# Chunked gated DeltaNet scan: solving for the residue of values and state product instead of for keys and values apart, with the keys' sums in other banks

## What is computed

```python
m = where(strict, (kb @ k.T) * decay, 0)          # kb = k * beta
a = m + eye(L)
sol = triangular_solve(a, [v * beta, kb * exp(G)])
w_val, k_cd = sol[:dv], sol[dv:]
def step(st):                                      # chunk after chunk
    v_new = w_val - k_cd @ st
    o = (q * exp(G)) @ st + attn @ v_new
    st = st * g_tot + k_tail.T @ v_new
```

## Time and profile before

| | |
|---|---|
| runs | 3146.82 us median of 3 (3145.96 to 3149.22) |
| the profiled execution | 3142.87 us, of which 3141.1 us are the span shown |
| busy in the span | PE 96%, PEld 92%, DVE 51%, POOL 35%, ACT 23% |
| granted clock of PE, mean | 0.981 of full speed |
| the scan | about 1821 to 2191 us of the span |

### The profile page before, as it was taken

One profiled execution on the slowest core, in us unless ns is written; L12 is line 12 of the kernel. 1 busy time (PEld: TensorE's weight loads), 2 busy tenths in 40 slices (PEclk: granted clock), 3 DMA queues, 4 the chain that ended last, 5 costly groups with the idle time before them and its releaser, 6 DMA issues. The chain is left out here.

```text
span 3141.1 us, 52954 instructions
## 1 busy us (share of the span) xinstructions
PE 3009.7 (96%) x22592; PEld 2885.3 (92%) x22592; DVE 1595.7 (51%) x2718; ACT 722.8 (23%) x1413; POOL 1089.4 (35%) x731
## 2 busy tenths in 40 slices
PE   8999999999999999999999969996999999999995
PEld 7999668999999999999999958885999999999995
DVE  2338665744444334478666645563473344433456
ACT  2213473310110100123221235553121001101012
POOL 2233101253222332327532147774452322322330
PEclk9999999999999999999999989997999999999998
DMA  6120102011111111114323134321311111111111
GB/s 173 45 62 7 48 1 85 14 54 45 43 41 41 48 54 48 41 28 126 98 84 97 59 104 110 89 69 54 94 39 41 54 48 41 43 46 41 48 41 57
DMA packets 265152, 185.48 MB, mean 59 GB/s; under 512 B 49833, under 2 KB 249879, under 8 KB 264919
## 3 DMA queue, kind: packets, MB, share of 16 engines
q1 hardware_dynamic: 264919, 182.11, 19.7%
HBM read 148.24 MB, written 33.84 MB: 58 GB/s over the span
## 5 line engine op out<-in xcount | busy, mean ns | idle before, releaser
L148 PE MATMUL ps<-xhi,whi 128*128 128x364 f32 (+1 forms) x3504 | 1159.7, 331 | 18.8 <-POOL wlo L1417 15.0
L149 PE MATMUL ps<-xlo,whi 128*128 128x364 f32 (+1 forms) x3504 | 1154.6, 330 | 0.0
L154 PE MATMUL ps<-xhi,wlo 128*128 128x364 f32 (+1 forms) x3504 | 1153.6, 329 | 0.0
L148 PEld LDWEIGHTS ps<-xhi,whi 128*128 128x128 f32 (+1 forms) x3504 | 659.1, 188 | 24.1 <-POOL wlo L1417 16.6
L149 PEld LDWEIGHTS ps<-xlo,whi 128*128 128x128 f32 (+1 forms) x3504 | 659.5, 188 | 3.2 <-issue 0.3
L154 PEld LDWEIGHTS ps<-xhi,wlo 128*128 128x128 f32 (+1 forms) x3504 | 658.8, 188 | 1.4
L1414 POOL TENSOR_SCALAR whi<-wraw 128x1024 fp32r<-128x1024 f32 x168 | 189.7, 1129 | 1235.6 <-PE ps L154 1235.3
L1980 DVE TENSOR_TENSOR z<-ps,z 128x364 f32<-128x364 f32 x432 | 232.0, 537 | 575.2 <-PE ps L154 575.2
L1417 POOL TENSOR_TENSOR wlo<-wraw,whi 128x1024 fp32r<-128x1024 f32 x168 | 431.6, 2569 | 14.0
L148 PE MATMUL ps<-eo_hhi,whi 128*128 128x364 f32 x528 | 174.5, 331 | 0.0
L148 PE MATMUL ps<-oo_hhi,whi 128*128 128x364 f32 x528 | 174.2, 330 | 0.0
(11 more groups left out here) (405 smaller groups left out, 4408.3 us busy)
## 6 DMA issues: line engine op xcount, KB each, us to landing
wraw<-in_w_ff_in SPq DMA_DIRECT2D x88, 512.0 KB, 3.7
wraw<-in_w_ff_out SPq DMA_DIRECT2D x44, 512.0 KB, 3.4
qkvz<-eo_ob SPq DMA_DIRECT2D x32, 546.0 KB, 4.6
wraw<-in_w_in_o SPq DMA_DIRECT2D x32, 512.0 KB, 4.5
z<-residual SPq DMA_DIRECT2D x6, 1456.0 KB, 8.2
wraw<-in_w_in_e SPq DMA_DIRECT2D x17, 512.0 KB, 3.9
residual<-z SPq DMA_DIRECT2D x3, 1456.0 KB, 6.7
dn_gb<-gates SPq DMA_DIRECT2D x34, 128.0 KB, 3.4
```

Of the source, the lines that this page charges most:

```text
L148: one = pe.matmul(out, whi, xhi, start=start, stop=False)
L149: two = pe.matmul(out, whi, xlo, start=False, stop=False)
L154: return pe.matmul(out, wlo, xhi, start=False, stop=stop)
```

## The change

It replaces the two products at the stage's end. Instead of TT applied to scaled keys and to scaled values, the recurrence forms the residue r = v - (k exp(G)) S first (DVE, `residue`), applies TT to it (PE, `solve`), and multiplies by beta (DVE, `new_values`). beta therefore sits in the rows of `upl`/`ups` and the columns of `low` differently (POOL's `pre` swaps two factors). The scaled keys `kc` are made by POOL (`scaled_keys`) from the normalised keys and `eg`. ACT copies the turned values in one instruction into `vt`. TT, `vt` and `kc` are double. The keys' sums go to banks 4 and 5, the turned values to 6 and 7. Ln of B's output norm is taken at level 3 (`root_o`), Exp and `normed` at level 4, and Exp for the mask `upi` is moved from level 2 to 3. The setup of `bcol` is dropped. The diff, cut, with eight columns of indentation removed:

```diff
-kbg, vb, kc, vn, Sg = (sb(n, [P, H, P]) for n in ("kbg", "vb", "kc", "vn", "Sg"))
+vt = (sb("vt0", [P, H, P]), sb("vt1", [P, H, P]))
+kc = (sb("kc0", [P, H, P]), sb("kc1", [P, H, P]))
+vn, Sg = (sb(n, [P, H, P]) for n in ("vn", "Sg"))
 ktl = (sb("ktl0", [P, H, P]), sb("ktl1", [P, H, P]))
 S = (sb("S0", [P, H, P]), sb("S1", [P, H, P]))
 egl = sb("egl", [P, 2, 2, H])
+TT = (TT, sb("TT1", [P, H, L]))
...
-            sp.wait_ge(s("ups_b"), A.th(1, 1))
+            sp.wait_ge(s("low_b"), A.th(1, 1))
...
+            sp.wait_ge(s("kc"), A.th(1, 1))
...
+    def scaled_keys(A):
+
+        pool.wait_ge(s("kn"), A.th(1, 1))
+        pool.wait_ge(s("eg"), A.th(1, 1))
+        if A.k >= 2:
+            pool.wait_ge(s("kS"), A.th(-2, 2))
+        for b, r in enumerate(A.blocks()):
+            ins = pool.tensor_tensor(kc[A.odd][:, :, r].rearrange("p (g hh) c -> p g hh c", g=2),
+                                     kk[:, b].rearrange("p hh g c -> p g hh c"),
+                                     eg[:, b].rearrange("p (g hh) c -> p g hh c", g=2), ALU.mult)
+        ins.then_inc(s("kc"), 1)
+
     def run(A, B, C):
         if B:
             decayed(B, 0)
         if A:
+            scaled_keys(A)
             levels_of(A, (1,))
...
-        pe.wait_ge(s("Tv"), B.th(1, 1))
+        if not B.first:
+
+            pe.wait_ge(s("oln"), B.th(0, 1))
...
+    def solve(B, b):
+
+        pe.wait_ge(s("r"), B.th(b + 1, 2))
+        pe.wait_ge(s("TT"), B.th(B.group(LEVELS - 1, b), 2 * LEVELS))
+        for h, half, j in places(b):
+            ins = pe.matmul(bank2(0)[half, j, :], TT[B.odd][half, j, :], vt[B.odd][half, j, :], start=True, stop=True)
+        ins.then_inc(s("Tr"), 1)
...
-            pe.wait_ge(s("vb"), A.th(1, 1))
+            pe.wait_ge(s("kln"), A.th(1, 1))
...
-                ins = pe.matmul(bank2(6)[:, HALVES[b], :], m.ones[:, :], sq[:, HALVES[b], :],
+                ins = pe.matmul(bank2(4)[:, HALVES[b], :], m.ones[:, :], sq[:, HALVES[b], :],
                                 start=True, stop=True)
             ins.then_inc(s("ksum"), 1)
             pe.wait_ge(s("in2"), A.loaded())
             if not A.first:
-                pe.wait_ge(s("kc"), A.th(0, 1))
-            turn(A, 4, kv, "vturned")
+                pe.wait_ge(s("TT"), A.th(0, 2 * LEVELS))
+            turn(A, 6, kv, "vturned")
         if B:
             old_values(B, 0)
+            solve(B, 0)
         if A:
             pe.wait_ge(s("kn"), A.th(1, 1))
+            pe.wait_ge(s("vt"), A.th(1, 1))
             gram_k(A)
...
             old_values(B, 1)
+            solve(B, 1)
...
-                    pe.wait_ge(s("kbg"), A.th(1, 1))
...
-            pe.wait_ge(s("vb"), A.th(1, 1))
-            if B:
-
-                pe.wait_ge(s("oln"), B.th(1, 1))
-            for b in range(A.nb):
-                pe.wait_ge(s("TT"), A.th(A.group(LEVELS - 1, b), 2 * LEVELS))
-                settle(pe, s("settled_pe"))
-                for h, half, j in places(b):
-                    ins = pe.matmul(bank1(4 + h // GR)[:, j, :], kbg[half, j, :], TT[half, j, :],
-                                    start=True, stop=True)
-            ins.then_inc(s("kcd"), 1)
-            for b in range(A.nb):
-                for h, half, j in places(b):
-                    ins = pe.matmul(bank2(0)[half, j, :], TT[half, j, :], vb[half, j, :], start=True, stop=True)
-            ins.then_inc(s("TvP"), 1)
...
-    def decays(C):
+    def decays_low(C):
         J = C.J
         act.wait_ge(s("clip"), C.th(1, 2))
         act.activation(low[:, 0:J], low[:, 0:J], ACT.Exp, scale=-1.0).then_inc(s("dlow"), 1)
+
+    def decays_up(C):
+        J = C.J
         act.wait_ge(s("clip"), C.th(2, 2))
         act.activation(upi[:, 0:J], upi[:, 0:J], ACT.Exp).then_inc(s("dup"), 1)
...
-    def rms(B):
+    def root_o(B):
         n = B.n
         act.wait_ge(s("osum"), B.th(1, 1))
         act.wait_ge(s("eps"), 1)
         act.activation(rt[:, :, 0:n], bank2(0, n), ACT.Ln, bias=m.eps[:, 1:2]).then_inc(s("oln"), 1)
+
+    def rms(B):
+        n = B.n
         act.wait_ge(s("oln"), B.th(1, 1))
         act.activation(rt[:, :, 0:n], rt[:, :, 0:n], ACT.Exp, scale=-0.5).then_inc(s("orms"), 1)
...
-            act.activation(rt[:, 0:A.J, :], bank2(6)[:, 0:A.J, :], ACT.Ln, bias=m.eps[:, 0:1])\
+            act.activation(rt[:, 0:A.J, :], bank2(4)[:, 0:A.J, :], ACT.Ln, bias=m.eps[:, 0:1])\
...
-            for j in range(A.J):
-                ins = act.mul(vb[:, j, :], bank2(4)[:, j, :],
-                              m.gcol[:, bass.ds(A.index, 1), H + j:H + j + 1].squeeze(1))
-            ins.then_inc(s("vb"), 1)
+            if A.k >= 2:
+
+                act.wait_ge(s("Tr"), A.th(-2, 2))
+            act.copy(vt[A.odd][:, 0:A.J, :], bank2(6)[:, 0:A.J, :]).then_inc(s("vt"), 1)
...
-            act.wait_ge(s("kturned"), A.th(1, 1))
-            if A.first:
-                act.wait_ge(s("bcol"), 1)
-            if B:
-
-                act.wait_ge(s("vn"), B.th(B.nb, 2))
-            for b in range(A.nb):
-                act.wait_ge(s("kscaled"), A.th(b + 1, 2))
-                settle(act, s("settled_act"))
-                for j in range(GR * b, GR * (b + 1)):
-                    ins = act.mul(kbg[:, j, :], bank2(6)[:, j, :],
-                                  m.bcol[:, bass.ds(A.index, 1), j:j + 1].squeeze(1))
-            ins.then_inc(s("kbg"), 1)
...
-                if B and l == 3:
+                        decays_low(C)
+                if l == 3:
+                    if C:
+                        decays_up(C)
+                    if B:
+                        root_o(B)
+                if B and l == 4:
                     rms(B)
...
-            act.wait_ge(s("kcd"), A.th(1, 1))
-            for g in range(2):
-                ins = act.copy(kc[:, HALVES[g], 0:n].rearrange("p h (b c) -> p h b c", c=L),
-                               bank1(4 + g)[:, 0:A.J, :].rearrange("p (b h) c -> p h b c", h=GR))
-            ins.then_inc(s("kc"), 1)
-
-            act.wait_ge(s("TvP"), A.th(1, 1))
-            act.copy(kbg[:, 0:A.J, :], bank2(0)[:, 0:A.J, :]).then_inc(s("Tv"), 1)
...
+        beta = m.gcol[:, bass.ds(B.index, 1), H + GR * b:H + GR * (b + 1)].squeeze(1).unsqueeze(2)
+        dve.wait_ge(s("Tr"), B.th(b + 1, 2))
+        dve.tensor_tensor(vn[:, hs, :], bank2(0)[:, hs, :], beta.to_broadcast([P, GR, P]), ALU.mult)\
+           .then_inc(s("vn"), 1)
+
+    def residue(B, b):
+
+        hs = HALVES[b]
+        v = vt[B.odd][:, hs, :]
+        dve.wait_ge(s("vt"), B.th(1, 1))
         dve.wait_ge(s("kS"), B.th(b + 1, 2))
-        dve.tensor_tensor(vn[:, hs, :], kbg[:, hs, :], bank2(0)[:, hs, :], ALU.subtract)\
-           .then_inc(s("vn"), 1)
+        dve.tensor_tensor(v, v, bank2(0)[:, hs, :], ALU.subtract).then_inc(s("r"), 1)
...
+            residue(B, 0)
             new_values(B, 0)
...
+            residue(B, 1)
+        if A:
+            dve.tensor_tensor(tt[:, 0:J], tt[:, 0:J], masked(m.EYE, J), ALU.add).then_inc(s("TT0"), 1)
+        if B and B.n == P:
             new_values(B, 1)
         if A:
-            dve.tensor_tensor(TT[:, 0:J], TT[:, 0:J], masked(m.EYE, J), ALU.add).then_inc(s("TT0"), 1)
...
-                if B and l == 3:
+                if B and l == 4:
                     normed(B)
```

More of the change, by code:

```diff
@@ L2342, in run @@
                     sp.wait_ge(s("kturned"), A.th(1, 1))
+                    settle(sp, s("settled_sp"))
+                    sp.wait_ge(s("kc"), A.th(1, 1))
                     settle(sp, s("settled_sp"))
@@ L2391, in pre @@
                 pool.wait_ge(s("low_m"), C.th(1, 1))
+                pool.tensor_tensor(low[:, 0:J], low[:, 0:J], GB[:, 1, 0:J], ALU.mult).then_inc(s("low_b"), 1)
+                pool.wait_ge(s("ups_m"), C.th(1, 1))
                 bt = m.gcol[:, bass.ds(C.index, 1), H:H + J].squeeze(1).unsqueeze(2).to_broadcast([P, J, L])
-                pool.tensor_tensor(low[:, 0:J], low[:, 0:J], bt, ALU.mult).then_inc(s("low_b"), 1)
-                pool.wait_ge(s("ups_m"), C.th(1, 1))
-                pool.tensor_tensor(ups[:, 0:J], ups[:, 0:J], GB[:, 1, 0:J], ALU.mult).then_inc(s("ups_b"), 1)
+                pool.tensor_tensor(ups[:, 0:J], ups[:, 0:J], bt, ALU.mult).then_inc(s("ups_b"), 1)
                 pool.tensor_tensor(upi[:, 0:J], upi[:, 0:J], masked(m.UPI, J), ALU.mult).then_inc(s("upi_m"), 1)
@@ L2469, in old_values @@
                 for h, half, j in places(b):
-                    ins = pe.matmul(bank2(0)[half, j, :], kc[:, h, r], S[b][:, h, :], start=True, stop=True)
+                    ins = pe.matmul(bank2(0)[half, j, :], kc[B.odd][:, h, r], S[b][:, h, :], start=True, stop=True)
                 ins.then_inc(s("kS"), 1)
@@ L2589, in run @@
                                 for h, half, j in places(b):
-                                    pe.matmul(bank1(6 + b)[half, j - GR * b, :], TT[half, j, :], X[half, j, :],
+                                    pe.matmul(bank1(6 + b)[half, j - GR * b, :], TT[A.odd][half, j, :], X[half, j, :],
```

(30 more changed lines are left out.)

2 lines of the change are left out of this document (removed).

## The result

| | before | after |
|---|---|---|
| runs | 3149.51 us median of 6 (3145.96 to 3150.59) | 3173.57 us median of 6 (3173.29 to 3176.15) |
| the profiled execution | 3142.87 us, span 3141.1 | 3175.59 us, span 3173.8 |
| ratio of the runs | | 1.0079, 95% interval 1.0068 to 1.0089 |

The change makes the kernel 24.1 us slower by the medians. Forecast were 24.9 us more and 3171.7 us; the median of before, over six runs now, is 2.7 us above the one that the forecast started from.

A forecast was written before the change was run, and what follows sets the result against it. The prediction took POOL's closed loop of 37.98 us a stage as the bound. Start -4.6, chain +14.5, clock +9.6 and end +5.4 made 24.9 us slower: median 3171.7 us, range 3158 to 3185.

The forecast's parts named there:

- The bound: Scan stage: POOL's loop closes at 37.98 us and is full; PE's loop is as long within half a microsecond.
- The chain, 2.4 us a stage: From Ln of the key sums to `osum_in`: residue and solves lengthen it, 2.4 us more in each of six full stages.
- The clock, 1.6 us a stage: Scan's full stages: PE idle about 4.5 us before `solve` lowers its clock, costing 1.6 us in each of six.
- The rival with twice the stretch: Full stages: half clock for twice as long, 3.3 us a stage, 3181.9 us in all; chance 0.12.
- The start: Stage 0 loses the two products and most of a wait for ACT; first `osum_in` comes 4.6 us earlier.
- Stage 8, "nothing, give or take 2": Half-size stage: about 1.8 us gained from the missing L2728 against about as much for two solves.
- the cover that I had counted for full stages: `normed` behind level 4 ends about half a microsecond before POOL reaches `ofull`; without this margin it adds directly.
- The end, 5.4 us: Stage 8's norm 2.7 us later, plus 2.7 us in the drain for a half-clock solve and `new_values`.
- The sum: Whole kernel: start, chain, clock and end together make it 24.9 us slower.

The follow-up runs named there:

- experiment 7: Kernel before with the stage-end keys' product (L2607) left out but for two matmuls, `kc` not computed: 3144.43 us, ratio to before 0.9983.
- experiment 8: Kernel before with a buffer of its own for the key norm: 3148.45 us, ratio to before 0.9995.
- experiment 9: Kernel before with POOL's last mask instruction (L2398) done twice in every stage: 3156.07 us, ratio to before 1.002.
- experiment 10: Changed kernel with own buffer for the key norm, residue(B, 0) ahead of the scaling of keys, output norm back at level 3: 3134.35 us, ratio to before 0.9956.
- experiment 5: Changed kernel with three matmuls of unused result between Ln of the key sums and the first solve: 3169.29 us, ratio to before 1.0065.
- experiment 2: Changed kernel with DVE's residue(B, 0) ahead of the scaling of A's keys instead of behind it: 3160.67 us, ratio to before 1.0044.
- experiment 3: Changed kernel with the output norm back at level 3 and the mask's Exp at level 2: 3169.8 us, ratio to before 1.0071.
- experiment 1: Changed kernel with a buffer of its own for the key norm, so Ln no longer waits for `olo`: 3152.71 us, ratio to before 1.0013.
- experiment 4: Changed kernel with five matmuls of unused result between Ln of the key sums and the first solve: 3182.65 us, ratio to before 1.0109.

## Why the prediction was right, point by point

*The bound.* Two loops of nearly one length, POOL's full: right, by experiments 7, 8 and 9. No run of the kernel before shortened both loops at once; of the changed kernel experiment 10 did, and its stage is 37.0 us. The rule of the Trainium skill's page "Perfetto Trace Analysis", section "Identifying the Most-Contended Engine", pointed at PE. Its weight loads were busy 83% against POOL's 75%, and yet experiments 7 and 9 speak for the chain.

*The chain, 2.4 us a stage.* Right. Where the clock is kept, the stage is 40.45 us (experiment 5) against 40.40, and the reordering that takes solve off this chain brings 1.7 us a stage back (experiment 2).

*The clock, 1.6 us a stage.* Right in kind and nearly in size: 1.36 in the stage shown, 1.4 by experiment 5. One reading under it was loose: in the first stage's row PE did not run "the following 3.3 us" at 0.50. It went on at 1863.95 at full clock, and the stretch at 0.50 began 1.9 us later. In the changed kernel the clock had fallen when PE went on, or fell within 1.1 us, so here the slow stretch met the chain. The rival with twice the stretch is what two stages show, the first full one and stage 8, each with 6.8 us. Six stages grew by 23.1 us in the profiles; the terms gave 24.1.

*The start.* From the first Ln of pair 0 to the first `osum_in` the profiles have 1888.17 - 1833.51 = 54.7 before and 1885.94 - 1836.35 = 49.6 after: 5.1 us less, forecast 4.6.

*Stage 8, "nothing, give or take 2".* This term was wrong: the interval before pair 7's `osum_in`, from the end of stage 7 into stage 8, grew from 33.97 (2151.26 - 2117.29 in the profile of before) to 2176.63 - 2138.12 = 38.51, 4.5 us. Two parts were left out of it. POOL's masks for pair 8 are half size, so it reached stage 7's `ofull` early and waited 2.87 us for the norm that now stands behind level 4 (the row at 2152.55): the cover that I had counted for full stages was missing. That used up the gain of 1.8 us from the missing L2728: Ln starts 20.47 us after pair 6's `osum_in`, where it was 19.96. And I had put the loss of clock into six stages only, while PE's hole is there too, 4.14 us: from Ln to `osum_in` it is 18.04 us for 14.01, 4.0 more where I had counted 1.8 for two solves. PE worked at 0.50 from 2161.6 to 2165.7 there; half of these 4.1 us is, as an estimate, the 2.2 that were not counted. Experiment 3 gives 2.3 us of the 4.5 back in its profile.

*The end, 5.4 us.* From pair 7's `osum_in` to the end of the last `olo` it is 45.5 us after (2176.63 to 2222.14) and 39.7 before: 5.8. PE in the drain of the changed kernel:

```profile
2200.48 1.97 PE L2489 MATMUL ps<-dn_S,dn_kc 128*64 128x128 f32 x16 [10.70 <-DMA dn_S<-in_state_delta]
...
2205.99 1.97 PE L2503 MATMUL ps<-dn_vt,dn_TT 64*64 64x128 f32 x16
2208.76 2.08 PE L2513 MATMUL ps<-dn_vn,dn_ktl 64*128 64x128 f32 x16 [0.79 <-DVE dn_vn L2754]
```

From L2489 to the state step L2513 it is 8.28 us, with the solve at half clock between, where 5.51 were before: 2.8 us, forecast 2.7.

*The sum.* The scan, from the first Ln to the end of the last `olo`, grew by 28.3 us in the two profiles: 23.1 + 4.5 + 5.8 - 5.1. The forecast was 24.9, so it was low by the 4.5 of stage 8. The medians differ by only 24.1, so that the forecast fits them better than it fits the scan's profile; the 4 us between are not accounted for. That the total came within 0.8 us of the medians is therefore partly luck: a term was short by 4.5 us, and something that these runs do not show made up for it. Runs of the kernel before spread from 3143.9 to 3156.7 us in all groups, and a profile shows one of them. Of the two profiles' difference of 32.7 us, 4.4 lie outside the scan: the first Ln alone comes 2.8 us later in after's profile, in code that was not changed.

## What to carry to other kernels

Follow a repeated stage back through every engine until the chain closes on itself, and add it up against the period: a loop that closes on the period bounds the stage, and an engine busy 95% beside it may have nothing to give. Before work is moved to save it on the busiest engine, look what the moved step waits for and what waits behind it in its queue; here putting one subtraction behind one multiplication cost 12.9 of the 24.1 us (experiment 2). A buffer that two steps share is a dependence between two stages, and it costs only when the loop through it is the longest one.

## What the runs showed of the hardware

A hole in PE's work costs twice, once idle and once in clock. After 3.68 us idle PE ran for about 3.4 us at 0.50, beginning 0.5 us after it went on; behind holes of 4.1 to 4.3 us it went on at 0.50 already. The matmuls in that stretch were on the chain: 1.4 us of a stage. How long the hole was did not settle it alone. In experiment 1 the clock stayed at 1.00 in the stages with holes of 0.85 to 1.33 us and fell after those of 1.79 and 1.80; in experiment 4 it fell once after 1.32 us (the first fill of a full stage took 6.25 us for 4.56). Matmuls without use that kept PE going held the clock at 1.00 in all six full stages of experiment 5; in experiment 4, where they were 1.5 us too long, they cost more than the clock gave back. A float32 matmul of 512 columns was recorded as two instructions of 0.46 us each (ten in 4.56 us), where I had counted one.
